# Four buffers for cached keys, later loads of cached values, and smaller constants in a decoder layer's attention

## The chip, the cores and the metric

One core of a Trainium2 chip. The metric is the time of one execution on the device, in microseconds (us).

## The reference, cut to what matters

One layer of a decoder with a prompt of 512 tokens and 8 sequences of 8 new tokens each, which have 2048 cached positions. All is float32.

```
x <- LN1(alpha*x + 0.5*gate1 * SwiGLU_1(mod1(x)))
x <- LN2(alpha*x + gate2 * W_o [mixA(h) ; mixB(h)]),  h = mod2(x)
x <- LN3(alpha*x + 0.5*gate3 * SwiGLU_2(mod3(x)))
```

Mixer A has 8 heads of 64 and reads keys and values at three strides (1 within 128, 4 within 512, 16 within 2048); mixer B is differential attention, 4 heads, whose cached keys and values lie in pages of 128 positions that a page table names. The cached keys and values of both mixers are read from memory once for each sequence.

## The kernel before, in words

The layer runs as stages: modulation vectors, feed-forward 1, the q/k/v projection, attention, output projection, feed-forward 2. The five engines run their own instruction lists and meet at semaphores. All transfers of the attention stage are issued by SyncE on one queue, in program order.

**The attention stage** goes over the 8 sequences of new tokens (0 to 7); each has 8 quarters, `i` = 0 to 7. Quarters 0 to 3 are mixer A's cached positions, 4 to 7 mixer B's. A quarter's load, of keys or of values, is one of these:

- quarters 0 and 1: four tiles of 96 far positions, one transfer of 768 KB
- quarters 2 and 3: two tiles of 128 near positions, one transfer of 512 KB
- quarters 4 to 7: four pages, four transfers of 256 KB. For these `load` (L1114) first reads four page numbers into registers (`value_load`, L1118), then waits, then issues four times.

The document calls the loads of quarter i K(i) and V(i), or K0 to K7 and V0 to V7, and those of quarters 4 to 7 paged, the others window loads.

For each quarter TensorE (`attend_tensor`, L1321 on) does, in this order: turn the keys, two of four feature blocks (`turn_keys`, L1221); a prompt score (L1292); turn the softmax weights of the quarter five back (`turn_weights`, L1260); turn the other two blocks of keys (L1221), after which `d_kt` stands at 4 for each quarter; turn prompt weights (L1303); multiply the weights of the quarter five back with its values (`values`, L1274, counted by `d_pv`); scores with the turned keys (L1233); every fourth quarter, prompt values (L1317). So V(i) is read five quarters after K(i): V5 in quarter 2 of the next sequence, V6 in quarter 3, V7 in quarter 4, V0 in quarter 5 of its own. ScalarE and VectorE copy turned keys out of PSUM (L1368, L1442), VectorE masks and takes maxima (L1450, L1482), ScalarE exponentiates and copies turned weights (L1373, L1396). GpSimd lays out queries (L1180, L1189). Prompt attention runs alongside, mixer A's heads in sequences 0 to 3 and mixer B's in 4 to 7.

**SyncE's queue** (`attend_sync`, L1108 to L1156): place after place it issues K(q), then V(q - 5), q counting quarters through all sequences. Keys and values have two buffers each, by the parity of the quarter. K(q) waits until the keys of q - 2 are turned, V(q - 5) until the values of q - 7 are done:

```
if is_v:
    eng.wait_ge(sem("d_pv"), q - 1)
else:
    eng.wait_ge(sem("d_kt"), 4 * q - 4)
```

Between K1 and the next load of sequence 0 it loads the masks of the new tokens (`new_ab`, L1149, 4096 bytes for each partition: 8 sequences by 64 columns, for 2 mixers). VectorE waits for them before its first quarter (L1549). Mixer B's cached scores have no mask; their bias operand is a tile of zeros of 512 columns (L1480). GpSimd clears `QB`, `QP` and `zeros` (L1160 to L1163), `QB` ahead of the stage, the others once the projection is done.

Of the kernel before, what the change touches and what calls it, by code (L numbers as in the profile page):

```python
# [19 lines left out]
ds = bass.ds  # L20

P = 128
# [4 lines left out]
NB = 8  # L27
# [31 lines left out]
SW = PAST + NSM  # L59


def constants():
# [24 lines left out]
    new = np.full((P, 2, NB, NSM), MASKED, np.float32)  # L87
    own = query - np.arange(NS)[None, :]
    for b in range(NB):
        new[:, 0, b, b * NS:(b + 1) * NS] = log_count(own)  # L90
        new[:, 1, b, b * NS:(b + 1) * NS] = np.where(own >= 0, 0.0, MASKED)
# [6 lines left out]
def build(nc, x_prompt, x_sample, c_prompt, c_sample, win_k, win_v, diff_k, diff_v, page_table, ln_g, ln_b,  # L98
# [3 lines left out]
    with ExitStack() as ctx:  # L102
# [67 lines left out]
        QB, o = place("QB", [P, 2, 4, 32], offset=o)  # L170
# [4 lines left out]
        new_ab, o4 = place("new_ab", [P, 2, NB, NSM], offset=o3)  # L175
        o = max(o, o4)
        kv01, o = place("kv01", [P, 2, 4, QW], offset=o)
        ropet, o = place("ropet", [P, PT_ + 1, 2, E // 2], offset=o)
# [3 lines left out]
        assert o <= fend  # L182
        kv23, o = place("kv23", [P, 2, 4, QW], offset=hreg)
        KC, o = place("KC", [P, 4, QW], offset=o)
        S0, o = place("S0", [P, SW], offset=o)
        On, o = place("On", [P, P], offset=o)
        zeros, o = place("zeros", [P, NPR], offset=o)
        part, o = place("part", [P, 4, NS], offset=o)
        assert o <= hend
        S1, o = place("S1", [P, SW], offset=treg)  # L190
        assert o <= hreg
        S = (S0, S1)

# [3 lines left out]
        assert o <= wreg[1]  # L197
        PP, o = place("PP", [P, 4, NPR], offset=wreg[1])
        QP, o = place("QP", [P, 2, 2, P], offset=o)
        assert o <= wreg[2]  # L200
        PTp1, o = place("PTp1", [P, PT_, NPR], offset=wreg[2])
        VH1, o = place("VH1", [P, PT_, P], offset=o)
        assert o <= treg
# [3 lines left out]
        def kv(slot):  # L207
            return kv01[:, slot] if slot < 2 else kv23[:, slot - 2]
# [825 lines left out]
        def landed_at(b, m, c):  # L1034

            before = sum(DMAS[k][j] for k in range(2) for j in range(4) if j % 2 == c % 2 and (k, j) <= (m, c))
            return 16 * (b * sum(DMAS[k][j] for k in range(2) for j in range(4) if j % 2 == c % 2) + before)
# [70 lines left out]
        def attend_sync():  # L1108
# [5 lines left out]
            def load(b, i, is_v):  # L1114
# [6 lines left out]
                if positive(q - 1):  # L1121
                    if is_v:
                        eng.wait_ge(sem("d_pv"), q - 1)
                    else:
                        eng.wait_ge(sem("d_kt"), 4 * q - 4)
                slot = kv(2 * is_v + c % 2)
                s = sem(f"{'kv'[is_v]}_landed{c % 2}")
# [12 lines left out]
            def body(b, run):  # L1140
                for i in quarters(b):
                    if alive(b):
                        load(b, i, 0)
                    if isinstance(b, int) and b == 0 and i == 1:
# [4 lines left out]
                        eng.dma_start(new_ab[:].rearrange("p a b c -> p (a b c)"), new_ab_d).then_inc(sem("new_masks"), 16)  # L1149
                    vb, vi = back(b, i, LAG)  # L1150
# [4 lines left out]
            eng.wait_ge(sem("pages"), 16)  # L1155
            each_sequence(body)  # L1156

        def attend_pool():
            eng = nc.gpsimd
            eng.memset(QB[:], 0.0).then_inc(sem("d_zero"), 1)  # L1160
            eng.wait_ge(qkv.used, 24)
            eng.memset(QP[:], 0.0).then_inc(sem("d_zero"), 1)
            eng.memset(zeros[:], 0.0).then_inc(sem("d_zero"), 1)  # L1163
# [40 lines left out]
        def attend_tensor():  # L1204
# [7 lines left out]
            def turn_keys(b, i, f):  # L1212
# [3 lines left out]
                if f == 0:  # L1216
                    pe.wait_ge(sem(f"k_landed{c % 2}"), landed_at(b, m, c))
                if positive(2 * q + f // 2):
                    pe.wait_ge(sem("d_kcv" if f % 2 else "d_kca"), 2 * q + f // 2)
                for k in range(nt):  # L1220
                    mm = pe.transpose(ps[:, f % 2, k * kw:(k + 1) * kw], kv(c % 2)[0:kw, k, f * P:(f + 1) * P], ident[0:kw, 0:kw])  # L1221
# [41 lines left out]
            def values(b, i):  # L1263
                m, c = divmod(i, 4)
                u = 2 * b + m
                pe.wait_ge(sem(f"v_landed{c % 2}"), landed_at(b, m, c))
# [3 lines left out]
                for k in range(CH[m][c]):  # L1270
                    tile = tile0(m, c) + k
                    kw = keys_of(m, tile)
                    for f in range(4):
                        mm = pe.matmul(ps[32 * f:32 * f + 32, 4, 0:P], PTd[0:kw, tile, 32 * f:32 * f + 32],  # L1274
                                       kv(2 + c % 2)[0:kw, k, f * P:(f + 1) * P], start=(tile == 0), stop=(tile == sum(CH[m]) - 1),
# [474 lines left out]
```

## Time and profile before

| | |
|---|---|
| median of 3 runs | 1698.56 us (1693.17 to 1702.2) |
| the profiled execution | 1696.01 us, its span 1694.2 us |
| TensorE busy | 1521.1 us, 90% of the span |
| VectorE, ScalarE, GpSimd busy | 666.9, 510.0, 65.7 us |
| attention stage | about 720 to 1150 us |
| transfers of the whole program | 245.71 MB, mean 145 GB/s |
| granted TensorE clock, mean | 0.963 |

The profile shows one execution. TensorE's busy time counts its matmuls, whose ends are modelled; an idle stretch is given in square brackets before the instruction that ended it, with what released it. A wait that is not on TensorE costs time only if TensorE waits for what comes of it.

### The profile page before, as it was taken

How to read it: one execution, taken by the hardware profiler on the slowest of the kernel's cores; microseconds unless marked ns; L12 is line 12 of the kernel's file. 1: busy time of each engine (PE TensorE's matmuls, PEld its weight loads, DVE VectorE, ACT ScalarE, POOL GpSimd, SP SyncE). 2: the span in 40 equal slices, each digit the busy share in tenths (PEclk: the TensorE clock that was granted, in tenths of full speed). 3: DMA queues.
4: the chain of work that ended last, by engine and by line, in shares of the span. 5: the costliest groups of instructions: out<-in, count | busy, mean ns of one | idle time of the engine just before them, and what ended most of it. 6: DMA issues, size and time to landing. Idle time of an engine off the chain costs nothing.

```text
span 1694.2 us, 31954 instructions
## 1 busy us (share of the span) xinstructions
PE 1521.1 (90%) x12575; PEld 1332.2 (79%) x12575; DVE 666.9 (39%) x1333; ACT 510.0 (30%) x835; POOL 65.7 (4%) x162
## 2 busy tenths in 40 slices
PE   4899999989998999878888878877899999989996
PEld 2788999989996767655655555546799999989995
DVE  0322323322435523345555545645642322322334
ACT  2422222221123222234444344443342222221122
POOL 0100000000002000000000000000010000000000
PEclk8899999989998999989999999987989999999998
DMA  9994222223222232378899998863212222223211
GB/s 335 388 317 128 75 87 80 81 81 86 77 70 77 66 118 75 101 217 264 265 279 265 260 274 253 269 209 101 75 50 87 75 86 84 76 71 101 82 57 57
DMA packets 212323, 245.71 MB, mean 145 GB/s; under 512 B 8512, under 2 KB 152378, under 8 KB 209155
## 3 DMA queue, kind: packets, MB, share of 16 engines
q1 hardware_dynamic: 212226, 244.42, 47.1%
q8 instruction: 61, 1.00, 0.2%
q14 instruction: 36, 0.29, 0.1%
HBM read 237.31 MB, written 7.08 MB: 144 GB/s over the span
## 4 chain that ended last, share of the span: by engine, by line
PE 77%; DMA 6%; DVE 5%; SPq 4%; issue 4%; ACT 3%; ACTq 0%; DVEq 0%
PE ps L290 52%; PE ps L932 10%; DMA kv<-in_cache_diff_k_dram 3%; PE ps L1274 2%; DMA wada<-in_w_ada_dram 2%; PE ps L1221 2%; SPq L1138 2%; PE ps L1233 2%; PE ps L714 2%; PE ps L1317 2%; PE ps L272 2%; SPq L1118 2%; DVE PP L1450 1%; DVE KC L1442 1%; PE ps L1292 1%
## 5 line engine op out<-in xcount | busy, mean ns | idle before, releaser
L257 ACT ACTIVATE whi<-w 128x1024 fp32r<-128x1024 f32 (+1 forms) x152 | 170.9, 1128 | 777.6 <-PE ps L290 663.6
L263 DVE TENSOR_TENSOR wlo<-w,whi 128x1024 fp32r<-128x1024 f32 (+1 forms) x152 | 199.8, 1317 | 413.4 <-ACT whi L257 412.9
L290 PE MATMUL ps<-hhi,whi 128*128 128x288 f32 x1472 | 317.9, 298 | 9.1 <-DVE wlo L263 5.4
L290 PE MATMUL ps<-hhi,wlo 128*128 128x288 f32 x1472 | 316.3, 297 | 0.0
L290 PE MATMUL ps<-hlo,whi 128*128 128x288 f32 x1472 | 316.1, 296 | 0.0
L290 PEld LDWEIGHTS ps<-hhi,whi 128*128 128x128 f32 x1472 | 238.0, 190 | 15.3 <-DVE wlo L263 6.2
L290 PEld LDWEIGHTS ps<-hlo,whi 128*128 128x128 f32 x1472 | 238.1, 189 | 0.0
L290 PEld LDWEIGHTS ps<-hhi,wlo 128*128 128x128 f32 x1472 | 238.1, 189 | 0.0
L290 PE MATMUL ps<-ffhi,whi 128*128 128x288 f32 x704 | 152.5, 299 | 12.3 <-DVE wlo L263 12.3
L1221 PEld LDWEIGHTS ps<-ident,kv 128*128 128x128 f32 (+1 forms) x896 | 97.5, 145 | 74.4 <-issue 58.0
L290 PE MATMUL ps<-fflo,whi 128*128 128x288 f32 x704 | 151.7, 297 | 0.0
L290 PE MATMUL ps<-ffhi,wlo 128*128 128x288 f32 x704 | 151.7, 297 | 0.0
L1221 PE MATMUL ps<-ident,kv 128*128 128x128 f32 (+1 forms) x896 | 120.7, 275 | 31.9 <-DMA kv<-in_cache_diff_k_dram 16.0
L290 PEld LDWEIGHTS ps<-ffhi,whi 128*128 128x128 f32 x704 | 114.7, 191 | 13.1 <-issue 13.1
L290 PEld LDWEIGHTS ps<-fflo,whi 128*128 128x128 f32 x704 | 114.8, 191 | 0.0
L290 PEld LDWEIGHTS ps<-ffhi,wlo 128*128 128x128 f32 x704 | 114.6, 191 | 0.0
L663 DVE TENSOR_TENSOR tmp<-tmp,ps 128x576 f32<-128x576 f32 x44 | 33.2, 755 | 202.7 <-PE ps L290 201.2
L1442 DVE COPY KC<-ps 128x512 f32<-128x512 f32 (+2 forms) x128 | 75.4, 589 | 95.1 <-PE ps L1221 66.0
L1274 PE MATMUL ps<-kv,PTd 128*32 128x128 f32 (+1 forms) x1792 | 67.3, 282 | 49.8 <-ACT PTd L1396 31.8
L1368 ACT ACTIVATE KC<-ps 128x512 f32<-128x512 f32 (+2 forms) x128 | 65.2, 509 | 141.0 <-PE ps L1221 141.0
L932 PE MATMUL ps<-whi,hhi 128*128 128x512 f32 (+1 forms) x240 | 96.7, 403 | 8.4 <-ACT hlo L361 5.5
L1274 PEld LDWEIGHTS ps<-kv,PTd 128*32 128x32 f32 (+1 forms) x1792 | 45.5, 111 | 67.3 <-ACT PTd L1396 32.1
(197 smaller groups left out, 1695.3 us busy)
## 6 DMA issues: line engine op xcount, KB each, us to landing
w<-in_ffn_w_in_dram SPq DMA_DIRECT2D x88, 512.0 KB, 3.8
wada<-in_w_ada_dram SPq DMA_DIRECT2D x18, 2048.0 KB, 13.2
kv<-in_cache_diff_k_dram SPq DMA_DIRECT2D x128, 256.0 KB, 4.8
kv<-in_cache_diff_v_dram SPq DMA_DIRECT2D x128, 256.0 KB, 3.6
w<-in_ffn_w_out_dram SPq DMA_DIRECT2D x32, 704.0 KB, 4.7
w<-in_w_qkv_dram SPq DMA_DIRECT2D x24, 512.0 KB, 3.6
kv<-in_cache_win_k_dram SPq DMA_DIRECT2D x16, 768.0 KB, 6.1
kv<-in_cache_win_v_dram SPq DMA_DIRECT2D x16, 768.0 KB, 8.8
```

What stands on the lines that cost most here:

```text
L257: nc.scalar.activation(whi[:, slot, 0:w], w32[:, slot, 0:w], ACT.Copy).then_inc(ph.hi, 1)
L263: nc.vector.tensor_tensor(wlo[:, slot, 0:w], w32[:, slot, 0:w], whi[:, slot, 0:w].bitcast(F32), ALU.subtract).then_inc(ph.lo, 1)
L272: m = nc.tensor.matmul(ps[:, banks + h, 0:TH], w, x[:, kk, h * TH:(h + 1) * TH], start=(kk == 0 and n == 0), stop=(kk == kall - 1 and n == 2))
L290: m = pe.matmul(ps[:, banks + h, 0:TH], w, x[:, kk, h * TH:(h + 1) * TH], start=(kk == 0 and n == 0), stop=(kk == kall - 1 and n == 2))
L714: m = pe.matmul(ps[32 * j:32 * j + 32, 4 + i % 2, 0:256], cT[:, k, :], wada[n % 4][:, k % 4, j * 256:(j + 1) * 256], start=(k == 0), stop= ...
L932: m = pe.matmul(ps[0:n, qkv_bank(g, t), :], x[:, kk, t * P:t * P + n], w, start=(kk == 0 and n3 == 0), stop=(kk == DB - 1 and n3 == 2))
L1118: page = [eng.value_load(pages[0:1, ds(b * NPAGE + tile + k, 1)], min_val=0, max_val=diff_k.shape[1] - 1) for k in range(n)]
L1138: eng.dma_start(slot[:, k, :], src).then_inc(s, 16)
L1221: mm = pe.transpose(ps[:, f % 2, k * kw:(k + 1) * kw], kv(c % 2)[0:kw, k, f * P:(f + 1) * P], ident[0:kw, 0:kw])
L1274: mm = pe.matmul(ps[32 * f:32 * f + 32, 4, 0:P], PTd[0:kw, tile, 32 * f:32 * f + 32], kv(2 + c % 2)[0:kw, k, f * P:(f + 1) * P], start=(ti ...
L1368: eng.activation(KC[:, f, 0:w], ps[:, 0, 0:w], ACT.Copy).then_inc(sem("d_kca"), 1)
L1442: eng.tensor_copy(KC[:, f, 0:w], ps[:, 1, 0:w]).then_inc(sem("d_kcv"), 1)
```

## The change

Keys get four buffers, one for each of the four quarters of a mixer, each with a semaphore of its own, and K(q) waits for the keys of q - 4. Values keep two buffers; V(q - 7) stands behind K(q) in SyncE's queue where V(q - 5) stood, and its wait, for the values of the quarter two before its own, is the same. The tile of zeros gives way to one zero column read with stride 0; the new tokens' masks are kept once, padded, and each sequence reads a shifted window of them, so that the load has 960 bytes for each partition. `QB` and `QP` move into memory that the rotated tiles leave, and are cleared by GpSimd once those are turned and stored. The attention stage's buffers are laid out anew.

```diff
--- before.py
+++ after.py
@@ -57,6 +57,7 @@
 A_CHUNKS = (4, 4, 2, 2)
 B_CHUNKS = (4, 4, 4, 4)
 SW = PAST + NSM
+NEWW = 2 * NSM - NS
 
 
 def constants():
@@ -84,11 +85,10 @@
     keys = np.concatenate([far, near])
     query = (np.arange(P) % NS)[:, None]
     past = log_count(PAST + query - keys[None, :])
-    new = np.full((P, 2, NB, NSM), MASKED, np.float32)
+    new = np.full((P, 2, NEWW), MASKED, np.float32)
     own = query - np.arange(NS)[None, :]
-    for b in range(NB):
-        new[:, 0, b, b * NS:(b + 1) * NS] = log_count(own)
-        new[:, 1, b, b * NS:(b + 1) * NS] = np.where(own >= 0, 0.0, MASKED)
+    new[:, 0, NSM - NS:NSM] = log_count(own)
+    new[:, 1, NSM - NS:NSM] = np.where(own >= 0, 0.0, MASKED)
     return {
         "ident": np.eye(P, dtype=np.float32), "rope": rope.reshape(P, -1),
         "mask_a": log_count(delta), "mask_b": causal, "past_a": past, "new_ab": new.reshape(P, -1),
@@ -167,45 +167,41 @@
         QT, o = place("QT", [P, 8, T], offset=freg)
         KT, o = place("KT", [P, 8, T], offset=o)
         V, o = place("V", [P, 2, PT_ + 1, QW], offset=o)
-        QB, o = place("QB", [P, 2, 4, 32], offset=o)
         PTo = o
         rot, o = place("rot", [P, PT_ + 1, QW], offset=o)
         rab, o = place("rab", [P, 2, QW], offset=o)
         PTd, o3 = place("PTd", [P, NPAGE + 1, P], offset=PTo)
-        new_ab, o4 = place("new_ab", [P, 2, NB, NSM], offset=o3)
-        o = max(o, o4)
-        kv01, o = place("kv01", [P, 2, 4, QW], offset=o)
-        ropet, o = place("ropet", [P, PT_ + 1, 2, E // 2], offset=o)
+        new_ab, o3 = place("new_ab", [P, 2, NEWW], offset=o3)
+        QB, o3 = place("QB", [P, 2, 4, 32], offset=o3)
+        QP, o3 = place("QP", [P, 2, 2, P], offset=o3)
+        On, o3 = place("On", [P, P], offset=o3)
+        part, o3 = place("part", [P, 4, NS], offset=o3)
+        assert o3 <= o
+        k0, o = place("k0", [P, 4, QW], offset=o)
+        k1, o = place("k1", [P, 4, QW], offset=o)
         mask_a, o = place("mask_a", [P, NPR], offset=o)
         mask_b, o = place("mask_b", [P, NPR], offset=o)
         past_a, o = place("past_a", [P, A_KEYS], offset=o)
-        assert o <= fend
-        kv23, o = place("kv23", [P, 2, 4, QW], offset=hreg)
+        ropet, _ = place("ropet", [P, PT_ + 1, 2, E // 2], offset=o)
+        k3, o = place("k3", [P, 4, QW], offset=o)
+
+        PTp0, o = place("PTp0", [P, PT_, NPR], offset=wreg[0])
+        VH0, o = place("VH0", [P, PT_, P], offset=o)
+        PP, o = place("PP", [P, 4, NPR], offset=o)
+        PTp1, o = place("PTp1", [P, PT_, NPR], offset=o)
+        VH1, o = place("VH1", [P, PT_, P], offset=o)
+        S1, o = place("S1", [P, SW], offset=o)
+        v0, o = place("v0", [P, 4, QW], offset=o)
+        v1, o = place("v1", [P, 4, QW], offset=o)
         KC, o = place("KC", [P, 4, QW], offset=o)
         S0, o = place("S0", [P, SW], offset=o)
-        On, o = place("On", [P, P], offset=o)
-        zeros, o = place("zeros", [P, NPR], offset=o)
-        part, o = place("part", [P, 4, NS], offset=o)
+        k2, o = place("k2", [P, 4, QW], offset=o)
         assert o <= hend
-        S1, o = place("S1", [P, SW], offset=treg)
-        assert o <= hreg
         S = (S0, S1)
-
-
-        PTp0, o = place("PTp0", [P, PT_, NPR], offset=wreg[0])
-        VH0, o = place("VH0", [P, PT_, P], offset=o)
-        assert o <= wreg[1]
-        PP, o = place("PP", [P, 4, NPR], offset=wreg[1])
-        QP, o = place("QP", [P, 2, 2, P], offset=o)
-        assert o <= wreg[2]
-        PTp1, o = place("PTp1", [P, PT_, NPR], offset=wreg[2])
-        VH1, o = place("VH1", [P, PT_, P], offset=o)
-        assert o <= treg
         sqf, o = place("sqf", [P, DB, T], offset=freg)
         ytok, o = place("ytok", [P, PT_ + 1, D], offset=freg)
 
-        def kv(slot):
-            return kv01[:, slot] if slot < 2 else kv23[:, slot - 2]
+        k_slots, v_slots = (k0, k1, k2, k3), (v0, v1)
 
         ps = ctx.enter_context(nc.psum_tensor("ps", [P, 8, 512], F32))
 
@@ -1031,7 +1027,11 @@
         def chunk_keys(m, c):
             return CH[m][c] * keys_of(m, tile0(m, c))
 
-        def landed_at(b, m, c):
+        def k_landed_at(b, m, c):
+
+            return 16 * (b * (DMAS[0][c] + DMAS[1][c]) + DMAS[0][c] + m * DMAS[1][c])
+
+        def v_landed_at(b, m, c):
 
             before = sum(DMAS[k][j] for k in range(2) for j in range(4) if j % 2 == c % 2 and (k, j) <= (m, c))
             return 16 * (b * sum(DMAS[k][j] for k in range(2) for j in range(4) if j % 2 == c % 2) + before)
@@ -1118,13 +1118,14 @@
                     page = [eng.value_load(pages[0:1, ds(b * NPAGE + tile + k, 1)], min_val=0,
                                            max_val=diff_k.shape[1] - 1) for k in range(n)]
                 q = QUARTERS * b + i
-                if positive(q - 1):
-                    if is_v:
+                if is_v:
+                    if q > 1:
                         eng.wait_ge(sem("d_pv"), q - 1)
-                    else:
-                        eng.wait_ge(sem("d_kt"), 4 * q - 4)
-                slot = kv(2 * is_v + c % 2)
-                s = sem(f"{'kv'[is_v]}_landed{c % 2}")
+                    slot, s = v_slots[c % 2], sem(f"v_landed{c % 2}")
+                else:
+                    if q > 3:
+                        eng.wait_ge(sem("d_kt"), 4 * q - 12)
+                    slot, s = k_slots[c], sem(f"k_landed{c}")
                 if m == 0 and tile < A_FAR:
                     src = far[is_v][ds(b, 1), :, tile:tile + n, :].rearrange("a g j c -> (a g) j c")
                     eng.dma_start(slot[0:FARW, 0:n, :], src).then_inc(s, 16)
@@ -1138,7 +1139,7 @@
                         eng.dma_start(slot[:, k, :], src).then_inc(s, 16)
 
             def body(b, run):
-                for i in quarters(b):
+                for i in range(QUARTERS if alive(b) else LAG + 2):
                     if alive(b):
                         load(b, i, 0)
                     if isinstance(b, int) and b == 0 and i == 1:
@@ -1146,21 +1147,25 @@
                         eng.wait_ge(sem("qk_turned"), 4 * (PT_ + 1))
                         eng.wait_ge(sem("kept1"), 16 * (PT_ + 1))
                         eng.wait_ge(sem("kept4"), 16 * (PT_ + 1))
-                        eng.dma_start(new_ab[:].rearrange("p a b c -> p (a b c)"), new_ab_d).then_inc(sem("new_masks"), 16)
-                    vb, vi = back(b, i, LAG)
+                        eng.dma_start(new_ab[:].rearrange("p a c -> p (a c)"), new_ab_d).then_inc(sem("new_masks"), 16)
+                    vb, vi = back(b, i, LAG + 2)
                     if alive(vb):
                         load(vb, vi, 1)
 
             eng.wait_ge(qkv.used, 24)
             eng.wait_ge(sem("pages"), 16)
+            eng.wait_ge(sem("rot"), 8 * (PT_ + 1))
             each_sequence(body)
 
         def attend_pool():
             eng = nc.gpsimd
+            eng.memset(stat[:, 6:7], 0.0).then_inc(sem("d_zero"), 1)
+            eng.wait_ge(qkv.used, 24)
+            eng.wait_ge(sem("qk_turned"), 4 * (PT_ + 1))
+            for g in (1, 4):
+                eng.wait_ge(sem(f"kept{g}"), 16 * (PT_ + 1))
             eng.memset(QB[:], 0.0).then_inc(sem("d_zero"), 1)
-            eng.wait_ge(qkv.used, 24)
             eng.memset(QP[:], 0.0).then_inc(sem("d_zero"), 1)
-            eng.memset(zeros[:], 0.0).then_inc(sem("d_zero"), 1)
             eng.wait_ge(sem("d_zero"), 3)
             eng.wait_ge(sem("qk_copied"), 4 * (PT_ + 1))
             eng.wait_ge(sem("vout"), 2 * (PT_ + 1))
@@ -1214,11 +1219,11 @@
                 nt, kw = CH[m][c], keys_of(m, tile0(m, c))
                 q = QUARTERS * b + i
                 if f == 0:
-                    pe.wait_ge(sem(f"k_landed{c % 2}"), landed_at(b, m, c))
+                    pe.wait_ge(sem(f"k_landed{c}"), k_landed_at(b, m, c))
                 if positive(2 * q + f // 2):
                     pe.wait_ge(sem("d_kcv" if f % 2 else "d_kca"), 2 * q + f // 2)
                 for k in range(nt):
-                    mm = pe.transpose(ps[:, f % 2, k * kw:(k + 1) * kw], kv(c % 2)[0:kw, k, f * P:(f + 1) * P], ident[0:kw, 0:kw])
+                    mm = pe.transpose(ps[:, f % 2, k * kw:(k + 1) * kw], k_slots[c][0:kw, k, f * P:(f + 1) * P], ident[0:kw, 0:kw])
                 mm.then_inc(sem("d_kt"), 1)
 
             def scores(b, i):
@@ -1263,7 +1268,7 @@
             def values(b, i):
                 m, c = divmod(i, 4)
                 u = 2 * b + m
-                pe.wait_ge(sem(f"v_landed{c % 2}"), landed_at(b, m, c))
+                pe.wait_ge(sem(f"v_landed{c % 2}"), v_landed_at(b, m, c))
                 pe.wait_ge(sem("d_ptc"), 5 * u + c + 2)
                 if c == 0 and positive(2 * u):
                     pe.wait_ge(sem("d_out"), 2 * u)
@@ -1272,7 +1277,7 @@
                     kw = keys_of(m, tile)
                     for f in range(4):
                         mm = pe.matmul(ps[32 * f:32 * f + 32, 4, 0:P], PTd[0:kw, tile, 32 * f:32 * f + 32],
-                                       kv(2 + c % 2)[0:kw, k, f * P:(f + 1) * P], start=(tile == 0), stop=(tile == sum(CH[m]) - 1),
+                                       v_slots[c % 2][0:kw, k, f * P:(f + 1) * P], start=(tile == 0), stop=(tile == sum(CH[m]) - 1),
                                        tile_position=(0, 32 * f), skip_group_check=True)
                     if tile == 0:
                         for f in range(4):
@@ -1477,7 +1482,7 @@
             def top(b, i):
                 m, c = divmod(i, 4)
                 w, o = chunk_keys(m, c), key0(m, tile0(m, c))
-                bias = past_a[:, o:o + w] if m == 0 else zeros[:, 0:w]
+                bias = past_a[:, o:o + w] if m == 0 else stat[:, 6:7].to_broadcast([P, w])
                 eng.wait_ge(sem("d_sc"), QUARTERS * b + i + 1)
                 eng.tensor_tensor_reduce(out=S[m][:, o:o + w], in0=ps[:, 2, 0:w], in1=bias, scale=1.0, scalar=MASKED,
                                          op0=ALU.add, op1=ALU.max, accum_out=stat[:, 32 + c:33 + c]).then_inc(sem("d_smax"), 1)
@@ -1515,7 +1520,7 @@
                         evacuate(b, i, 3)
                         if c == 0:
                             eng.wait_ge(sem("d_snew"), u + 1)
-                            eng.tensor_tensor(S[m][:, o:o + NSM], ps[:, 5, 0:NSM], new_ab[:, m, ds(b, 1), :].rearrange("p a k -> p (a k)"),
+                            eng.tensor_tensor(S[m][:, o:o + NSM], ps[:, 5, 0:NSM], new_ab[:, m, NSM - NS - b * NS:2 * NSM - NS - b * NS],
                                               ALU.add).then_inc(sem("d_new"), 1)
                         prompt_norm(b, i, mixer_of(b, run))
                         if c == 1:
```

## Rows read from the trace of the kernel before

**Rows 1.** Windows of sequence 3: busy us (instructions) of PE, PEld, DVE, ACT, POOL; PEclk, DMA share, GB/s.

```profile
884.70:895.00 10.30, 8.00 (x120) 6.41 (x119) 6.01 (x21) 4.65 (x13) 0.97 (x3) 1.00 0.69 219
895.00:920.00 25.00, 20.13 (x243) 13.45 (x244) 12.48 (x37) 10.76 (x26) 1.29 (x6) 1.00 0.98 264
```

**Rows 2.** Waits, 700 to 1160 us: who waited for whom: us, times, longest.

```profile
PE ps L1221 <- DMA kv<-in_cache_diff_k_dram: 16.0, 11, 2.9
...
PE ps L1221 <- DMA kv<-in_cache_win_k_dram: 8.5, 2, 7.3
```

**Rows 3.** Timeline of TensorE, sequence 3: start, length, line, shapes, [idle before <- releaser].

```profile
869.36 0.88 PE L1221 MATMUL ps<-ident,kv 96*128 96x96 f32 x8
...
885.79 1.08 PE L1274 MATMUL ps<-kv,PTd 128*32 128x128 f32 x32 [1.09 <-ACT PTd L1396]
...
889.02 0.60 PE L1221 MATMUL ps<-ident,kv 128*128 128x128 f32 x4
...
891.16 1.08 PE L1274 MATMUL ps<-kv,PTd 128*32 128x128 f32 x32 [1.22 <-ACT PTd L1396]
...
896.00 1.08 PE L1274 MATMUL ps<-kv,PTd 128*32 128x128 f32 x32
...
900.38 1.09 PE L1221 MATMUL ps<-ident,kv 128*128 128x128 f32 x8 [2.44 <-DMA kv<-in_cache_diff_k_dram]
...
904.53 0.43 PE L1274 MATMUL ps<-kv,PTd 96*32 96x128 f32 x8 [1.00 <-ACT PTd L1393]
```

**Rows 4.** Timeline of SyncE's queue, sequence 3: start, time over which issued, how many.

```profile
869.51 1.91 SPq L1138 DMA_DIRECT2D kv<-in_cache_diff_v_dram  x4
...
884.66 1.90 SPq L1138 DMA_DIRECT2D kv<-in_cache_diff_k_dram  x4
888.96 1.88 SPq L1138 DMA_DIRECT2D kv<-in_cache_diff_v_dram  x4
893.24 1.88 SPq L1138 DMA_DIRECT2D kv<-in_cache_diff_k_dram  x4
895.17 0.43 SPq L1130 DMA_DIRECT2D kv<-in_cache_win_v_dram  x1
```

**Rows 5.** DMA issues at 890.5, 895.2, 1051.4 and 716.1 us: size, us to landing.

```profile
kv<-in_cache_diff_v_dram SPq DMA_DIRECT2D x1, 256.0 KB, 4.1
...
kv<-in_cache_win_v_dram SPq DMA_DIRECT2D x1, 768.0 KB, 8.2
...
kv<-in_cache_win_v_dram SPq DMA_DIRECT2D x1, 768.0 KB, 7.2
...
kv<-in_cache_win_k_dram SPq DMA_DIRECT2D x1, 768.0 KB, 8.3
```

**Rows 6.** Timeline of TensorE, sequence 6, columns as in rows 3.

```profile
1023.55 0.88 PE L1221 MATMUL ps<-ident,kv 96*128 96x96 f32 x8
...
1045.86 1.08 PE L1274 MATMUL ps<-kv,PTd 128*32 128x128 f32 x32 [1.06 <-ACT PTd L1396]
...
1052.13 1.08 PE L1274 MATMUL ps<-kv,PTd 128*32 128x128 f32 x32 [0.25 <-ACT PTd L1396]
...
1055.36 1.09 PE L1221 MATMUL ps<-ident,kv 128*128 128x128 f32 x8 [1.29 <-DMA kv<-in_cache_diff_k_dram]
...
1059.76 0.43 PE L1274 MATMUL ps<-kv,PTd 96*32 96x128 f32 x8 [1.13 <-ACT PTd L1393]
```

**Rows 7.** Timeline at the start of the stage: SyncE's queue, TensorE, VectorE.

```profile
716.67 0.36 SPq L1149 DMA_DIRECT2D new_ab<-in_new_ab_dram  x1
...
721.66 1.51 PE L1221 MATMUL ps<-ident,kv 96*128 96x96 f32 x8 [7.33 <-DMA kv<-in_cache_win_k_dram]
...
725.68 0.56 DVE L1442 COPY KC<-ps 128x384 f32<-128x384 f32 x1 [26.12 <-DMA new_ab<-in_new_ab_dram]
```

**Rows 8.** Groups of VectorE by line and shape: busy us, mean ns | idle before.

```profile
L1482 DVE CUSTOM_DVE_ANT_0 S<-ps,zeros 128x512 f32<-128x512 f32 x32 | 22.1, 692 | 49.8 <-PE ps L1233 49.8
...
L979 DVE TENSOR_TENSOR rab<-ps,ropet 128x512 f32<-128x512 f32 x8 | 5.5, 690 | 0.6
```

## The prediction

> **What bounds the kernel now.** The profile's busy line comes first (table above): TensorE is busy 90% of the span, so time comes from what makes TensorE wait or from its work, and the change leaves its work alone. The edits sit in the attention stage, about 720 to 1150 us, where one sequence takes about 51 us. Next the windows over one sequence: the DMA engines are loaded unevenly, 0.69 busy from 884.7 to 895 and 0.98 from 895 to 920, while TensorE is busy some four fifths of both [rows 1]. So neither is solid, and the table of waits must say what TensorE lacks: 16.0 us in 11 waits for cached keys of mixer B and 8.5 us in 2 for those of mixer A [rows 2]. The other waits of TensorE there are for ScalarE and VectorE inside a quarter, whose order stays. Of the 8.5 us, 7.3 is the stage's first load and stays [rows 7]. Keys therefore cost 24.5 - 7.3 = 17.2 us that the change can reach.
>
> Then the queue. K(i) and V(i) are the loads of quarter i. TensorE's values step of quarter i takes V(i-5). In sequence 3 TensorE starts quarter 0 at 869.36, and takes V6 at 891.16 (+21.80 from that start), V7 at 896.00 (+26.64) and V0 at 904.53, after standing 2.44 us for K5 [rows 3]. SyncE issues V4 at 869.51, K4 at 884.66, V7 at 888.96 and K5 at 893.24, each of four pages, and V0 at 895.17 [rows 4]. The last three paged loads are 4.30 and 4.28 us apart, and the waits ahead of them were over: V7's for the values step of quarter 2 (885.79, 1.08 long), K5's for the last key turn of quarter 3 (889.02, 0.60 long) [rows 3]. So **4.29 us is SyncE's own time for one paged load**: four issues fill 1.9 us of it, the rest is mostly reading page numbers. TensorE's wait for K5 is this: K4, V7 and K5 in a row, and K5 too late.
>
> **The change, part by part.** *Key loads two quarters earlier.* K(q) waits for the turns of q-4 instead of q-2. Every key has two quarters more. K(4) comes out at +4.4 instead of +15.3 (below) and K5, the one that TensorE stood for, at +13.0 instead of +23.9, wanted at 900.38 - 869.36 - 2.44 = +28.6 [rows 3]; so no key after the first is late: **-17.2 us**.
>
> *Value loads two places later in the queue.* Their gate (values two before are done) and the moment they are wanted are unchanged, and their place is now beside a key load that waits on the same TensorE quarter, so the gates alone cost nothing. But the mix changes. Before, paged values loads V4 to V7 stood in places 1 to 4 and paged keys in 4 to 7: most stand beside a window load of one issue, and only K4, V7 and K5 follow each other directly. Now V4 is in place 3 and K4,V5 / K5,V6 / K6,V7 / K7,V0 follow: **eight paged loads in a row**, V4 K4 V5 K5 V6 K6 V7 K7. V4's gate and place in time stay (+0.15; it was issued just behind a key load gated by quarter 7, and still is). At 4.29 each the rest come at K4 +4.4, V5 +8.7, K5 +13.0, V6 +17.3, K6 +21.6, V7 +25.9, K7 +30.2, and V0 1.93 behind K7 as now behind K5 [rows 4], +32.1. No gate is later than these, so SyncE's own time decides.
>
> A paged load is complete 5.7 us after its first issue: V7's last page is issued 1.55 in, between 890.4 and 890.7, and lands 4.1 later. V0 lands 8.2 us after its issue in sequence 3 and 7.2 in sequence 6 [rows 5]. I take 7.2: the 8.2 followed the slower K5 of the two. Sequence 3: V6 lands +23.0, wanted +21.8, **1.2 late**. V7 lands +31.6, wanted +26.6+1.2, **3.8 late**. V0 lands +39.3, wanted at 904.53 - 869.36 - 2.44 (K5's wait is gone) = +32.7, plus 5.0, **1.6 late**. Sum 6.6; with 8.2 it is 7.6. Sequence 6 starts at 1023.55, and V4 is again issued just behind that; quarters with mixer B's prompt heads reach values later: V6 wanted at +22.3 (0.7 late), V7 at +28.6 (2.3 late), V0 at 1059.76 - 1023.55 - 1.29 = +34.9, plus 3.0 (1.4 late) [rows 6]. Sum 4.4, or 5.4. What waits behind a late value: TensorE's scores of the same quarter and all later turns, so each of these moves the whole loop. Seven sequences (1 to 7) see it, three of the first kind and four of the second: 3 x 6.6 + 4 x 4.4 = **+37.4 us**. Without any stall at V0 it is 3 x 5.0 + 4 x 3.0 = 27.0; with 8.2 throughout, 44.4.
>
> The Trainium skill speaks against this term: DMA: Bandwidth & Descriptors, section Issuing engines are not separate DMA queues, says a sequencer's time to initiate DMAs "is usually small relative to the DMA itself". By it the 37.4 would be nothing and the sum 1677.9 us. The trace here does not agree: 4.29 us of SyncE for a load that is complete 5.7 us after its first issue.
>
> *Start of the stage.* VectorE stands until the new tokens' masks have landed, at about 725.6; they are issued at 716.67, half a microsecond behind K1 [rows 7], and K1 lands 8.3 us after its issue [rows 5], at 724.4. So 0.5 MB of masks costs 1.2 us there; a quarter of the bytes (960 instead of 4096 a partition) costs 0.3: **-0.9 us**. K2 and K3 are now issued right behind and could take that back: 0 is the other end. The added wait of SyncE for the rotated tiles is over long before.
>
> *Zeros.* The maximum over mixer B's scores reads one broadcast column instead of a 512-wide tile. It takes 692 ns now; a 512-wide operation that reads a broadcast table took 690 [rows 8]. No row has this custom instruction with a broadcast operand: the bounds are 2 ns less and, were it 10% more, 32 x 0.07 = 2 us. I take 0, by the nearest row. Clearing QB moves to the stage's start in place of the zeros tile, a smaller tile on GpSimd while the first keys are awaited (until 721.66 [rows 7]): 0. The new placements overlap only buffers whose last readers are done: 0. The end is unchanged: the last value loads have no key loads about them before or after.
>
> **Sum.** The profiled execution took 1696.0 us (span 1694.2 and 1.8 around it), 0.15% under the median 1698.56. 1696.0 - 17.2 + 37.4 - 0.9 = **1715.3 us**. Its own range: 1702 (27.0) to 1723 (44.4, no gain at the start).
>
> **Rivals.** *Faster: values are in time.* The seat is V7. It is in time in sequence 3 if six paged spacings fit in 26.64 - 5.7 - 0.15 = 20.8 us, so under 3.5 us each (3.8 in sequence 6). For it: all eight go with every wait over, and half of the 4.29 is register work. Against: the two spacings in [rows 4] already had their waits over. Time: 1696.0 - 17.2 - 0.9 = 1677.9. This is where the Trainium skill's sentence on issuing engines (DMA: Bandwidth & Descriptors) would lead.
>
> *Even.* A spacing of 3.9: V7 lands +29.3, 2.6 late in sequence 3 and 0.7 in sequence 6; V0 comes 2.7 earlier, 1.3 and 1.0 late: 3 x 3.9 + 4 x 1.7 = 18.5, against 18.1 saved: 1696.4. For it: little is needed. Against: the same two rows.
>
> *Slower still: the transfers themselves.* Behind K7 and V0 come K0 and V1 at once, while the engines are 0.98 busy already [rows 1]. At the stage's start K0 has landed by 721.66 and K1 by 724.4, so a window load holds the engines 2.8 us. If V0 shares with one such load it lands 2.8 later: 7 x 2.8 = 20, 1735. Against: these come behind V0, and K1 behind K0 shows them served in turn.
>
> *It does not do what it says*: keys are no earlier because SyncE is late. Not here: K5 at +13.0 is wanted near +28.6.
>
> **How the numbers follow.** Forecast 0.62, even 0.18, faster 0.14, slower still 0.06. The faster case and the slowest are left out of the range, 0.20; it holds the even case and the forecast's bounds with a little for sequences 4 and 5, whose quarters 2 and 3 are shorter: 1692 to 1727. 0.5% is 8.5 us, about what a measurement of this kernel can tell from no change. Faster 0.14, same 0.18, slower 0.68; the forecast's own lower edge lies within 8.5 us of before, but the weight of that case is above it.
>
> **What would show it.** TensorE's waits for keys gone except the first; in their place some 20 waits of the values line for `diff_v` and `win_v`, 1 to 4 us each, 37 in all, at quarters 3, 4 and 5. SyncE with eight groups of four issues 4.3 us apart in each sequence. A sequence about 53 to 55 us instead of 50 to 52. Wrong, if the spacing is under 3.8 us, if value waits sum to less than 18 us, or if the masks' arrival moves by more than 2 us.

## The result and the profile after

The changed kernel takes 1755.43 us (median of 4 runs, 1749.97 to 1758.81), the kernel before on the same chip 1699.5 us; the ratio is 1.0321, 95% interval 1.0277 to 1.0365. It is slower, as forecast, but by 56 us where 19 were forecast, and the time lies above the range of 1692 to 1727. The profiled execution has a span of 1748.2 us, 54.0 more than before's 1694.2.

First TensorE's busy line, the slices with its granted clock, and its waits between 700 and 1220 us:

```profile
PE 1543.7 (88%) x12575; PEld 1344.9 (77%) x12575; DVE 667.4 (38%) x1333; ACT 510.4 (29%) x835; POOL 66.6 (4%) x162
...
PEclk9999999999999999898999899987989999999998
```

```profile
PE ps L1279 <- DMA v<-in_cache_diff_v_dram: 41.3, 15, 5.8
...
PE ps L1279 <- DMA v<-in_cache_win_v_dram: 24.2, 8, 3.5
PE ps L1279 <- ACT PTd L1401: 22.1, 25, 1.2
PE ps L1226 <- DMA k<-in_cache_win_k_dram: 7.6, 1, 7.6
...
PE ps L1279 <- ACT PTd L1398: 4.8, 6, 0.9
```

The same waits of the kernel before, of which [rows 2] showed the two for keys:

```profile
PE ps L1274 <- ACT PTd L1396: 31.8, 36, 1.2
...
PE ps L1274 <- ACT PTd L1393: 12.6, 13, 1.4
...
PE ps L1274 <- DMA kv<-in_cache_diff_v_dram: 3.2, 2, 3.1
```

The 54.0 us divide cleanly. TensorE's busy time rose by 1543.7 - 1521.1 = **22.6 us with the same 12575 matmuls**, and so its idle time by 31.4. Of the idle time, waits for keys fell from 24.5 to 7.6 (-16.9), waits for values rose from 3.2 to 65.5 (+62.3), and waits for ScalarE's copies of turned weights fell from 44.4 to 26.9 (-17.5), because a late value covers such a wait. That is +27.9; the other 3.5 are small groups.

Sequence 3 is the one of [rows 3] and [rows 4]. It starts at 887.68 now. SyncE's queue, start, time over which issued, how many:

```profile
887.82 1.90 SPq L1139 DMA_DIRECT2D v<-in_cache_diff_v_dram  x4
892.14 1.88 SPq L1139 DMA_DIRECT2D k<-in_cache_diff_k_dram  x4
896.44 1.88 SPq L1139 DMA_DIRECT2D v<-in_cache_diff_v_dram  x4
901.08 1.90 SPq L1139 DMA_DIRECT2D k<-in_cache_diff_k_dram  x4
905.38 1.88 SPq L1139 DMA_DIRECT2D v<-in_cache_diff_v_dram  x4
909.67 1.88 SPq L1139 DMA_DIRECT2D k<-in_cache_diff_k_dram  x4
913.96 1.88 SPq L1139 DMA_DIRECT2D v<-in_cache_diff_v_dram  x4
918.25 1.88 SPq L1139 DMA_DIRECT2D k<-in_cache_diff_k_dram  x4
920.18 0.43 SPq L1131 DMA_DIRECT2D v<-in_cache_win_v_dram  x1
```

The eight paged loads stand in a row, 4.3 us apart but for one gap of 4.64, and V7 comes at +26.28 where +25.9 was forecast. TensorE in the same sequence:

```profile
911.08 1.45 PE L1279 MATMUL ps<-v,PTd 128*32 128x128 f32 x32 [2.85 <-DMA v<-in_cache_diff_v_dram]
...
913.32 1.92 PE L1226 MATMUL ps<-ident,k 128*128 128x128 f32 x8
...
918.89 1.08 PE L1279 MATMUL ps<-v,PTd 128*32 128x128 f32 x32 [1.29 <-DMA v<-in_cache_diff_v_dram]
...
920.76 1.09 PE L1226 MATMUL ps<-ident,k 128*128 128x128 f32 x8
...
927.97 0.43 PE L1279 MATMUL ps<-v,PTd 96*32 96x128 f32 x8 [3.51 <-DMA v<-in_cache_win_v_dram]
```

V6, V7 and V0 are late, at quarters 3, 4 and 5, as forecast. The new thing is beside them. Eight turns of keys, 1.09 us at 920.76, take 1.92 us at 913.32, two microseconds after the first wait. Windows of the changed kernel (columns as in [rows 1]) say why:

```profile
905.00:909.00 4.00, 3.23 (x33) 2.05 (x21) 2.10 (x8) 1.28 (x4) 0.29 (x1) 1.00 0.74 239
909.00:913.00 4.00, 1.92 (x40) 1.43 (x40) 0.60 (x2) 1.05 (x3) 0.00 (x0) 0.83 0.77 192
913.00:917.00 4.00, 4.00 (x35) 3.43 (x31) 1.99 (x9) 1.21 (x4) 0.69 (x2) 0.74 0.78 287
917.00:921.00 4.00, 2.71 (x49) 1.64 (x47) 1.09 (x5) 2.73 (x5) 0.00 (x0) 1.00 0.68 244
```

The granted clock, third column from the right, falls from 1.00 (2.4 GHz) about the end of the wait, to 1.2 GHz for part of two windows, and comes back. Over the seven sequences with late values the mean is 0.92, over those of the kernel before 0.99:

```profile
768.00:1173.00 405.00, 314.12 (x3506) 212.65 (x3502) 193.10 (x627) 159.95 (x369) 25.98 (x90) 0.92 0.77 229
```

```profile
767.00:1120.00 353.00, 288.43 (x3506) 199.01 (x3502) 192.76 (x627) 159.80 (x369) 25.80 (x90) 0.99 0.90 267
```

The first is of after, the second of before: the same 3506 matmuls, 25.7 us more of TensorE. In windows of one microsecond the clock of the changed kernel falls to 1.2 GHz twice in each of the sequences 1 to 7, once about the waits for V6 and V7 and once about that for V0. It also falls once in sequence 0, which has a single late value: V0, waited for 2.66 us until 750.41. Scores of this form take 1.07 us at 743.70, and just behind that wait they take nearly double:

```profile
752.35 1.95 PE L1238 MATMUL ps<-KC,QB 128*32 128x512 f32 x8
```

### The profile page after: what moved, and what is told of

It is laid out like the page before. It is cut to its first block, busy times and chain, and to the rows that moved or that the text cites. A ratio compares the mean times of both kernels' runs of the same rounds, so it can differ in the third digit from the quotient of the medians.

```text
span 1748.2 us, 31956 instructions
## 1 busy us (share of the span) xinstructions
PE 1543.7 (88%) x12575; PEld 1344.9 (77%) x12575; DVE 667.4 (38%) x1333; ACT 510.4 (29%) x835; POOL 66.6 (4%) x162
## 4 chain that ended last, share of the span: by engine, by line
PE 73%; SPq 8%; DMA 7%; DVE 4%; issue 4%; ACT 2%; ACTq 0%; DVEq 0%
PE ps L286 50%; PE ps L928 10%; SPq L1139 4%; DMA v<-in_cache_win_v_dram 4%; SPq L1118 3%; PE ps L1279 2%; DMA wada<-in_w_ada_dram 2%; PE ps L1238 2%; PE ps L1226 2%; PE ps L710 1%; PE ps L1322 1%; DMA v<-in_cache_diff_v_dram 1%; PE ps L268 1%; PE ps L1297 1%; DVE PP L1455 1%
## 5 line engine op out<-in xcount | busy, mean ns | idle before, releaser
L286 PEld LDWEIGHTS ps<-hhi,whi 128*128 128x128 f32 x1472 | 237.9, 190 | 15.3 <-DVE wlo L259 6.2
L1279 PE MATMUL ps<-v,PTd 128*32 128x128 f32 (+1 forms) x1792 | 74.7, 304 | 94.0 <-DMA v<-in_cache_diff_v_dram 41.3
L1226 PEld LDWEIGHTS ps<-ident,k 128*128 128x128 f32 (+1 forms) x896 | 102.7, 150 | 60.5 <-issue 51.4
L1226 PE MATMUL ps<-ident,k 128*128 128x128 f32 (+1 forms) x896 | 127.1, 285 | 13.9 <-DMA k<-in_cache_win_k_dram 7.6
L1279 PEld LDWEIGHTS ps<-v,PTd 128*32 128x32 f32 (+1 forms) x1792 | 50.3, 119 | 112.4 <-issue 70.3
```

Of the source, the lines that this page charges most:

```text
L286: m = pe.matmul(ps[:, banks + h, 0:TH], w, x[:, kk, h * TH:(h + 1) * TH], start=(kk == 0 and n == 0), stop=(kk == kall - 1 and n == 2))
L1226: mm = pe.transpose(ps[:, f % 2, k * kw:(k + 1) * kw], k_slots[c][0:kw, k, f * P:(f + 1) * P], ident[0:kw, 0:kw])
```

## The experiments

All ratios are to the kernel before, run beside them on the same chip; e1 to e4 shared one chip and its runs of the kernel before, and so did e5 to e8 and e9 to e11.

| run | what it is | ratio | 95% interval |
|---|---|---|---|
| changed kernel | | 1.0321 | 1.0277 to 1.0365 |
| e1_after_held | changed, page numbers kept for values | 0.998 | 0.9956 to 1.0005 |
| e2_before_held | before, page numbers kept for values | 0.9944 | 0.9916 to 0.9973 |
| e3_after_fixed | changed, no page numbers read | 0.9866 | 0.9812 to 0.9919 |
| e4_small_parts | before, zeros and masks of the change | 1.0006 | 0.9983 to 1.0029 |
| e5_after_early | changed, page numbers read early | 0.9886 | 0.9855 to 0.9917 |
| e6_before_early | before, page numbers read early | 0.9896 | 0.9865 to 0.9927 |
| e7_place6 | changed, V(q-6) behind K(q) | 1.0092 | 1.0062 to 1.0121 |
| e8_before_twice | before, page numbers of values read twice | 1.0312 | 1.028 to 1.0344 |
| e9_filler | changed, filler work ahead of late values | 1.0199 | 1.0161 to 1.0238 |
| e10_place5 | changed, V(q-5) behind K(q) | 0.9973 | 0.9949 to 0.9998 |
| e11_place6_early | place six, page numbers read early | 0.9861 | 0.9824 to 0.9899 |

### Is it SyncE's reading of page numbers? (e1, e2, e3)

The theory is the prediction's: the values are late because SyncE spends 4.3 us on each of eight paged loads in a row. The rival is the transfers. e1 takes the reading away from value loads, by keeping the registers of the key load:

```diff
-                    page = [eng.value_load(...) for k in range(n)]
+                    page = held[i] if is_v else [eng.value_load(...) for k in range(n)]
+                    held[i] = page
```

> Changed kernel, but the four page numbers that SyncE reads for a paged key load stay in registers and the value load of the same quarter uses them, so a paged value load costs SyncE its four issues and no reading. SyncE theory (its 4.3 us for each of eight paged loads in a row make V6, V7 and V0 late): a paged load that follows a paged key load comes about 2.1 us after it instead of 4.3, V7 is issued near +19 of its sequence instead of +26 to +28, the waits for values fall from 62 us to under 10, TensorE's granted clock in the stage goes back to about 1.0, time 1678 to 1690. Rival (the 16 DMA engines are what is late, behind window loads of keys two quarters early): issue times move, landings hardly, time stays over 1735. Rival (something else in the new layout, such as where the buffers lie): over 1735 too, with waits for values gone.

e2 has the same edit on the kernel before.

> The same on the kernel before: two buffers for keys, values in their old place, paged value loads without reading page numbers. SyncE theory: K5 follows V7 as before but V7 follows K4 about 2.2 us sooner, so K5 is issued about 2 us earlier and most of the 17 us of waits for keys go: 1683 to 1692. Rival (those waits come from transfers that share the DMA engines): within 4 us of before.

e3 takes all reading away from the changed kernel; it gathers fixed pages of mixer B's cache:

```diff
-                    page = [eng.value_load(...) for k in range(n)]
+                    page = [(b * NPAGE + tile + k) * 5 // 4 for k in range(n)]
```

> Changed kernel with page numbers that are fixed when the program is built, so it reads no page table for cached keys and values of mixer B and gathers other pages; bytes and transfers are the same. SyncE theory: all paged loads about 2 us apart, no wait for values but some at V0, where transfers and no longer SyncE decide: 1675 to 1688, no more than 5 us from the run that keeps the registers. Rival (DMA engines): over 1735.

SyncE's queue in e3, one sequence, and TensorE's waits for values in e3:

```profile
869.68 1.75 SPq L1138 DMA_DIRECT2D k<-in_cache_diff_k_dram  x4
871.48 1.90 SPq L1138 DMA_DIRECT2D v<-in_cache_diff_v_dram  x4
```

```profile
PE ps L1278 <- DMA v<-in_cache_win_v_dram: 2.9, 2, 2.0
...
PE ps L1278 <- DMA v<-in_cache_diff_v_dram: 2.0, 1, 2.0
```

Paged loads now follow each other in 1.8 us where no gate stands between, and 65.5 us of waits for values become 4.9. As many bytes go through the same 16 DMA engines in the same order, so the transfers were not what was late. e1 recovers 3.4% of the 4.5% that e3 does, and stays above its expected time: key loads still read, so a pair of paged loads costs 6.2 to 6.5 us in sequence 3, and V0 is still late in most sequences. Its waits for values are 19.6 us, where under 10 were expected, and its TensorE is busy 1533.5 us, 12.4 more than before's 1521.1, so it still has part of the slower work too. In e1, SyncE in sequence 3, and TensorE's waits for values:

```profile
876.03 1.88 SPq L1142 DMA_DIRECT2D k<-in_cache_diff_k_dram  x4
878.01 1.80 SPq L1142 DMA_DIRECT2D v<-in_cache_diff_v_dram  x4
882.22 1.88 SPq L1142 DMA_DIRECT2D k<-in_cache_diff_k_dram  x4
```

```profile
PE ps L1282 <- DMA v<-in_cache_win_v_dram: 14.6, 7, 3.2
...
PE ps L1282 <- DMA v<-in_cache_diff_v_dram: 5.0, 4, 2.1
```

e2 gives 0.6% where I expected 0.4 to 1.0% (1683 to 1692 against 1699.5): part of before's waits for keys was SyncE's reading too.

### The small parts (e4)

```diff
-                bias = past_a[:, o:o + w] if m == 0 else zeros[:, 0:w]
+                bias = past_a[:, o:o + w] if m == 0 else stat[:, 6:7].to_broadcast([P, w])
```

and the masks of 960 bytes for each partition, in the kernel before.

> The kernel before with only the small parts of the change: zeros read from one broadcast column, masks of the new tokens in 960 bytes for each partition; loads, buffers and their order as before. My prediction priced them at -0.9 us together: within 3 us of before, the maxima over mixer B's scores at 692 ns as before, VectorE's first copy of the stage about 1 us earlier. Rival (the broadcast operand slows the maximum, or two readers of the masks' new layout): 5 us or more above before, with that instruction over 0.8 us.

No difference, as expected. In the changed kernel the maximum with the broadcast operand takes what it took [rows 8], and VectorE starts 723.30 - 720.18 = 3.1 us after TensorE's first turn, where it was 725.68 - 721.66 = 4.0 [rows 7]. The forecast of -0.9 us was right to the tenth, if too small for a timed run to show. Both rows are of the changed kernel:

```profile
L1487 DVE CUSTOM_DVE_ANT_0 S<-ps,stat x32: 691/692/693, 744.8 to 1179.1; 128x512 f32<-128x512 f32 x32
```

```profile
723.30 0.56 DVE L1447 COPY KC<-ps 128x384 f32<-128x384 f32 x1 [25.54 <-DMA new_ab<-in_new_ab_dram]
```

### Reading early, and how much the four buffers bring (e5, e6)

e3 gathers other pages, so e5 gets rid of the late reading with the right ones: SyncE reads each paged quarter's numbers in places 0 to 3, where its key loads are window loads, and `load` takes them from the kept registers for both loads (that part of the edit is left out here).

```diff
                     if alive(b):
                         load(b, i, 0)
+                    if alive(b) and i < 4:
+                        read_pages(b, i + 4)
```

> Changed kernel; each paged quarter's four page numbers are read once, behind the key load of the quarter four before (places 0 to 3, where SyncE has nothing but window loads), and kept for the key load and the value load. Computes what the changed kernel does. SyncE theory: paged loads 1.9 to 2.2 us apart where nothing gates them, as with fixed pages; ratio to before 0.983 to 0.992 (fixed pages gave 0.9866). Rival (fixed pages were fast because of which pages they gathered, not because SyncE had no reading to do): ratio near 0.998, as with kept registers.

> The kernel before (two buffers for keys, values five places back) with the same early reading of page numbers. SyncE theory: K5, now held up behind K4 and V7, comes at its gate, about 3.5 us sooner, no late keys but the first: ratio 0.984 to 0.992, so that four buffers for keys bring nothing over it. Rival (four buffers are needed as well, since transfers are late by themselves): waits for keys of 8 us or more stay and the ratio is 0.994 or above, like the kept registers' 0.9944.

Both beat the kernel before by over 1%, and they cannot be told apart. So e3's gain was not in its choice of pages. e5's queue and its waits for values (its only wait for keys is the first):

```profile
868.23 1.89 SPq L1143 DMA_DIRECT2D k<-in_cache_diff_k_dram  x4
870.21 1.80 SPq L1143 DMA_DIRECT2D v<-in_cache_diff_v_dram  x4
```

```profile
PE ps L1285 <- DMA v<-in_cache_win_v_dram: 2.2, 2, 1.2
...
PE ps L1285 <- DMA v<-in_cache_diff_v_dram: 1.5, 1, 1.5
```

and the waits of e6, with two buffers for keys:

```profile
PE ps L1227 <- DMA kv<-in_cache_win_k_dram: 10.6, 4, 7.0
PE ps L1227 <- DMA kv<-in_cache_diff_k_dram: 5.4, 6, 1.9
```

With two buffers 9.0 us of later waits for keys are left (10.6 + 5.4 less the first of 7.0), where I expected none, and 1.3 for values; with four buffers none for keys and 3.7 for values. So of e6's expectation the ratio held, 0.9896, and the absence of late keys did not. That the four buffers are worth a few microseconds is what these rows suggest; the timed runs do not show it.

### Where the value loads stand (e7, e10, e11)

```diff
-                    vb, vi = back(b, i, LAG + 2)
+                    vb, vi = back(b, i, LAG + 1)
```

is e7; e10 has `LAG` there, e11 is e7 with the early reading of e5.

> Changed kernel with value loads one place later than before instead of two (V(q-6) behind K(q)); page numbers read as in the changed kernel. SyncE theory, by the same chain with 4.3 to 4.5 us for a paged load: V7 issued near +22, 1 us late in sequences 1 to 3, V0 near +28, 1 to 2.5 us late; some 12 us of waits for values and 5 of lower clock against 17 saved on keys: ratio 0.996 to 1.005. Rival (the four key buffers, their early window loads or the new layout cost the 55 us, wherever the values stand): ratio 1.015 or more.

> Changed kernel with value loads in the place they had before, V(q-5) behind K(q), so that four buffers and the new layout are left of the change. SyncE theory: a key load stands in the queue behind a value load whose gate is the quarter two back, so keys gain one quarter at most, and K5 is still issued behind K4 and V7, less than 1 us earlier than before: ratio 0.994 to 1.002. Rival (layout, semaphores or early window loads cost time by themselves): 1.005 or more.

> Place six with page numbers read early, for the best of the orders: once SyncE is not late, the place should not matter, ratio 0.983 to 0.991, within the spread of places seven (0.9886) and five (0.9896). Rival (the order of the queue matters by itself, through the transfers): clearly outside these two.

e10 is the change without its move of the value loads: 0.9973. Four buffers, the new layout and the early window loads cost nothing that shows. One place later is 1.0092, two are 1.0321. With SyncE's reading out of the way the order stops mattering: 0.9886 for two places, 0.9861 for one. e7 came out above what I expected (1.005 at most). Its waits:

```profile
PE ps L1279 <- DMA v<-in_cache_win_v_dram: 22.6, 7, 4.8
PE ps L1279 <- DMA v<-in_cache_diff_v_dram: 11.1, 8, 3.1
```

33.7 us, where my chain gave 12. V0, a window load, is late by more than I let it be. The waits for ScalarE's turned weights fell from 44.4 to 36.4 us, so some 8 of the 33.7 are not new, which leaves about 26. TensorE is busy 1526.8 us, 5.7 more than in the kernel before. e10 still waits for paged keys as long as before (15.3 us against 16.0), so K5 stays late behind K4 and V7; its waits for window loads of keys are 13.4 us, where they were 8.5:

```profile
PE ps L1226 <- DMA k<-in_cache_diff_k_dram: 15.3, 11, 3.5
```

### More of the suspected cost, in the kernel before (e8)

```diff
+                    if is_v:
+                        page = [eng.value_load(...) for k in range(n)]
```

> The kernel before, with the page numbers of each paged value load read twice: 2.2 us more of SyncE for each, nothing else. SyncE theory: V7 and K5 of each sequence come 2.2 us later, waits for keys grow from 17 us to about 33, some waits for values appear, and TensorE's granted clock falls to its lower level after the longer ones: ratio 1.010 to 1.020. Rival (SyncE's reading is hidden behind its waits): ratio 0.998 to 1.003.

The direction is as expected and the size is not: 1.0312, as much as the whole change costs. The queue of its sequence 3, which starts at 886.19:

```profile
888.54 1.90 SPq L1141 DMA_DIRECT2D kv<-in_cache_diff_v_dram  x4
...
913.60 1.88 SPq L1141 DMA_DIRECT2D kv<-in_cache_diff_v_dram  x4
```

V7 is issued at 913.60, +27.4, where it was +19.6 in [rows 4]: not 2.2 but 7.8 us later. The delays of V4, V5, V6 and V7 add up, since the gates between them hardly hold SyncE up any more. Waits for paged keys grew as expected, from 16.0 to 35.2 us, but waits for paged values from 3.2 to 33.7, and TensorE is busy 1544.7 us, 23.6 more than before's 1521.1: the slower work is here too, with the layout of the kernel before. SyncE had less room than I thought: the kernel before stands close to the same edge that the change crosses.

### The clock (e9)

```diff
+                    if alive(b) and positive(b) and i in (3, 4, 5):
+                        pe.wait_ge(sem("d_out"), 4 * b - 2 * (i < 5))
+                        for _ in range(20):
+                            pe.transpose(ps[:, 4, 2 * P:3 * P], ident[:], ident[:])
                     if alive(lb):
                         values(lb, li)
```

The filler comes with one more wait of TensorE, until the bank of PSUM in which values are accumulated has been read. Its turns write an unused part of that bank, and the new tokens' attention sums of this run are not the right ones; how the filler reaches them was not looked into. The loads, their order and all other work are those of the changed kernel.

> Changed kernel; ahead of the values step of quarters 3, 4 and 5 of sequences 1 to 7, where TensorE stands for late values, it turns the unit matrix 20 times into a part of PSUM that nobody reads (about 2.7 us each time, 57 us in all, nearly all inside the 60 us of waits). Clock theory (the changed kernel loses some 20 us because the granted clock falls to 1.2 GHz after each of these waits and the work that follows runs at half speed): granted clock of the stage near 1.0 instead of 0.93, the waits shorter by the filler, time 8 to 20 us below the changed kernel, ratio to before 1.018 to 1.028. Rival (the slower matmuls come from the transfers, or the clock falls whatever TensorE does): ratio 1.032 or above, since the filler can only add.

1.0199: 420 matmuls were added and 1.2% of the time went away. A window over the seven sequences of e9, with 3506 + 420 matmuls, against the changed kernel's above:

```profile
766.00:1162.00 396.00, 336.76 (x3926) 244.58 (x3922) 192.26 (x627) 160.04 (x369) 25.82 (x90) 0.99 0.79 235
```

The clock is back at 0.99 from 0.92. TensorE's busy line and the filler's own group, L1354:

```profile
PE 1567.6 (90%) x12995; PEld 1375.6 (79%) x12995; DVE 666.3 (38%) x1333; ACT 510.2 (29%) x835; POOL 66.4 (4%) x162
```

```profile
L1354 PE MATMUL ps<-ident 128*128 128x128 f32 x420 | 49.3, 273 | 0.0
```

Without the filler TensorE is busy 1567.6 - 49.3 = 1518.3 us, no more than before's 1521.1. So the 22.6 us of slower work came from the clock, and the clock from TensorE standing idle for late values.

They are not all a price on top of the waits. Work that runs slower between a late V6 and a late V7 fills time in which TensorE would otherwise have waited for V7: from one values step to the next, without the wait, it takes 918.89 - 911.08 - 1.29 = 6.5 us in sequence 3, where it took 896.00 - 891.16 = 4.8 [rows 3]. In e9 filler and idle time together are 49.3 + (1737.3 - 1567.6) = 219.0 us, and the changed kernel's idle time is 204.5. Part of these 14.5 us more is filler that outlasted its wait, so how the 54.0 us would split with the clock kept up stays open; the filler gave back about 21 us of time (1.0321 - 1.0199, of 1700; by the two intervals, some 11 to 30).

## Why the prediction was wrong in size

- **The mechanism was right.** SyncE's own time, 4.29 us for a paged load, eight of them in a row, V6, V7 and V0 late, at quarters 3 to 5, in sequences 1 to 7: the queue and TensorE's waits after show each of them, and e1, e3 and e5, which spare SyncE's reading or move it, take most or all of the loss away. The forecast also had V7's issue nearly right, +26.28 for +25.9 in sequence 3. The sentence that a sequencer's time to initiate DMAs "is usually small relative to the DMA itself" (the Trainium skill, DMA: Bandwidth & Descriptors, Issuing engines are not separate DMA queues) would have led to 1677.9. The traces do not agree while SyncE reads page numbers between the loads: 4.3 us of it for each. With the reading moved (e5) two paged loads stand 2.0 us apart, and 0.9886 of 1699.5 is 1680, close to that sum.
- **Keys, -17.2 us**: measured -16.9.
- **Start, -0.9, and zeros, 0**: measured 0.9 and no change in the instruction.
- **Values, +37.4 us**: measured 62.3 of waits less 17.5 of ScalarE waits that they cover, **+44.8**. Two things go that way. V0 is late by 2.66 us in sequence 0 as well, which I had left out. And SyncE is slower than 4.29 in most sequences: from V4 to V7 it takes 26.1 to 27.9 us over the seven, where 25.7 were forecast. In sequence 1 the first two paged loads begin 5.5 us apart, some with issues that take 2.2 to 3.1 us instead of 1.9. What holds those issues up was not tried.

```profile
768.38 3.14 SPq L1139 DMA_DIRECT2D v<-in_cache_diff_v_dram  x4
773.92 1.88 SPq L1139 DMA_DIRECT2D k<-in_cache_diff_k_dram  x4
...
783.05 2.24 SPq L1139 DMA_DIRECT2D k<-in_cache_diff_k_dram  x4
```

- **The step that failed** is the one that said what waits behind a late value: "TensorE's scores of the same quarter and all later turns, so each of these moves the whole loop". It counted the waits and took the work after them to run as fast as before. It runs slower, by **+22.6 us** in all, and nothing in my sum stood for that: the prediction gives the granted clock no word. With it: -16.9 + 44.8 + 22.6 + 3.5 of small groups = 54.0, the difference of the spans; as said under e9, the split between waits and slower work is one of accounting. The profile of before could have warned. Its granted clock has a mean of 0.99 over seven sequences, but it falls to 1.2 GHz twice in them, once just behind a wait for K5 in sequence 4, where eight turns of keys take 1.57 us instead of 1.09:

```profile
950.66 1.57 PE L1221 MATMUL ps<-ident,kv 128*128 128x128 f32 x8 [2.18 <-DMA kv<-in_cache_diff_k_dram]
```

- **A slip in the range**: the lower edge of the forecast, with 27.0 for values, is 1696.0 - 17.2 + 27.0 - 0.9 = 1704.9 and not 1702. It changes nothing here.
- **The rivals**: faster needed a spacing under 3.5 us and even one of about 3.9, and the change has 4.3. The edits of e3 and e5 bring it to 1.8 to 2.0 where no gate stands between. The case of slower still put the loss in the transfers of V0; e3 shows the transfers in time. The time came out beyond that case, for another reason.

## What to carry to other kernels

Before loads are moved in a queue, add up the issuing engine's own time over the stretch in which they then stand together, reading of registers included: here it was the length of that chain, not the gates or the depth of the buffers, that said when the last of them started. Where the loop hangs on it, read table entries where the queue has nothing to do and keep them; here that gave 1.0 to 1.4% with either depth of buffers, more than any order of the loads gave. And look at the granted clock as well when a change adds waits of TensorE: here 31.4 us more of idle time came with 22.6 us of slower work.

## What was not expected of the hardware

- The granted clock fell from 2.4 to 1.2 GHz about waits of TensorE of a few microseconds, and filler matmuls inside the waits kept it up (0.92 without, 0.99 with them). The length of a single wait does not tell when: in the kernel before, it fell behind a wait of 2.18 us for K5 in sequence 4, and not behind those of 2.44 us in sequence 3 and 2.92 us in sequence 5; in the changed kernel it fell behind one of 2.66 us in sequence 0. What decides was not tried.
- 2.2 us more of SyncE for 32 value loads, 70 us spread over 400, cost 53 us (e8), 23.6 of them as slower work of TensorE. V7's issue moved by 7.8 us in sequence 3 for 2.2 us more at each of four loads, so SyncE's queue had little slack there.
- A broadcast operand of one column costs VectorE's custom maximum nothing, 692 ns for 512 columns either way.
